# The feed-forward tail of a hybrid trunk block: eleven pairs of hidden tiles in chunks of 2, 3, 3 and 3, one plain pair, and operand blocks loaded by ScalarE

## The reference, cut to what matters

```python
h = _modulated_norm(x, norm_ffn_g[l], shift2, scale2)
hid = _causal_dwconv(h @ w_up[l], ffn_conv_w[l], ffn_conv_b[l])   # 1024 -> 6144, conv(3)
act, val = jnp.split(hid, 2, axis=-1)
x = x + gate2[:, None, :] * ((jax.nn.gelu(act) * val) @ w_down[l])   # 3072 -> 1024
return _rmsnorm(x, norm_final_g)
```

## Time and profile before

| | before |
|---|---|
| median of 3 runs | 1510.73 us |
| profiled execution | 1510.02 us |
| its span | 1508.3 us |
| PE busy | 1493.7 us (99%) |
| DVE busy | 1252.7 us (83%) |
| ACT busy | 819.4 us (54%) |
| POOL busy | 406.3 us (27%) |
| HBM read, written | 167.95 MB, 61.87 MB |
| clock granted to PE | 0.999 of full speed |

### The profile page before, as it was taken

One profiled execution on the slowest core, in us unless ns is written; L12 is line 12 of the kernel. 1 busy time (PEld: TensorE's weight loads), 2 busy tenths in 40 slices (PEclk: granted clock), 3 DMA queues, 4 the chain that ended last, 5 costly groups with the idle time before them and its releaser, 6 DMA issues.

```text
span 1508.3 us, 19815 instructions
## 1 busy us (share of the span) xinstructions
PE 1493.7 (99%) x6794; PEld 1233.5 (82%) x6794; DVE 1252.7 (83%) x1584; ACT 819.4 (54%) x1237; POOL 406.3 (27%) x313
## 2 busy tenths in 40 slices
PE   7999999999999999999999999999999999999998
PEld 5888888888888888888888878888888888888887
DVE  7987888777777786799869999999999987777776
ACT  5368888634454363423436555555555553444447
POOL 0033434522213223000101133333333331333325
PEclk9999999999999999999999999999999999999999
DMA  9432133373543364572520244444444436777722
GB/s 369 180 111 60 57 91 96 126 266 109 163 140 121 109 216 147 190 233 80 175 70 29 66 164 157 156 157 152 150 153 153 154 112 233 252 251 251 251 67 113
DMA packets 212227, 231.12 MB, mean 153 GB/s; under 512 B 9920, under 2 KB 164896, under 8 KB 211360
## 3 DMA queue, kind: packets, MB, share of 16 engines
...
HBM read 167.95 MB, written 61.87 MB: 152 GB/s over the span
## 4 chain that ended last, share of the span: by engine, by line
PE 94%; DVE 4%; ACT 1%; issue 0%; DMA 0%; DVEq 0%; ACTq 0%
PE ps L907 75%; PE ps L987 6%; PE ps L1008 2%; PE ps L1300 1%; PE ps L1146 1%; PE ps L1281 1%; PE ps L1058 1%; PE ps L1203 1%; PE ps L1104 1%; DVE wop L1984 1%; DVE hq L2644 1%; DVE hidw L2701 1%; DVE n L2636 0%; PE ps L1093 0%; PE ps L1330 0%; PE ps L808 0%
## 5 line engine op out<-in xcount | busy, mean ns | idle before, releaser
L1376 ACT ACTIVATE wop<-raw 128x512 fp32r<-128x512 f32 (+1 forms) x541 | 307.1, 571 | 345.1 <-PE ps L907 231.4
L1984 DVE TENSOR_TENSOR wop<-raw,wop 128x512 fp32r<-128x512 f32 (+1 forms) x541 | 377.6, 702 | 103.1 <-ACT wop L1376 101.5
L733 POOL TENSOR_TENSOR raw<-raw,raw 128x512 f32<-128x512 f32 (+1 forms) x69 | 100.0, 1450 | 858.2 <-DVE wop L1984 394.8
L907 PE MATMUL ps<-hq,wop 128*128 128x512 f32 x888 | 213.7, 390 | 0.2 <-DVE hq L2644 0.2
L907 PEld LDWEIGHTS ps<-hq,wop 128*128 128x128 f32 x888 | 166.4, 188 | 36.2 <-DVE hq L2644 1.0
L907 PE MATMUL ps<-yq,wop 128*128 128x512 f32 x792 | 191.3, 390 | 0.0
L907 PE MATMUL ps<-dq,wop 128*128 128x512 f32 x840 | 190.6, 389 | 0.0
L907 PEld LDWEIGHTS ps<-dq,wop 128*128 128x128 f32 x840 | 157.7, 188 | 32.7
L907 PEld LDWEIGHTS ps<-yq,wop 128*128 128x128 f32 x792 | 148.0, 188 | 30.7
L1998 DVE TENSOR_TENSOR ps<-ps,snap_p 128x512 f32<-128x512 f32 x136 | 94.6, 695 | 44.5 <-PE ps L907 43.9
L1391 ACT ACTIVATE snap_p<-ps 128x512 f32<-128x512 f32 x136 | 81.2, 597 | 82.7 <-PE ps L907 82.7
...
## 6 DMA issues: line engine op xcount, KB each, us to landing
dq<-hid_keep SPq DMA_DIRECT2D x35, 1024.0 KB, 7.0
...
raw<-in_w_down SPq DMA_DIRECT2D x80, 128.0 KB, 2.3
...
quarter_ring<-in_w_ada SPq DMA_DIRECT2D x64, 128.0 KB, 2.2
```

The costliest lines, as they stand in the source:

```text
L733: nc.gpsimd.tensor_tensor(s1, a21, a22, ALU.add).then_inc(s_made, 1)
L907: done = nc.tensor.matmul(bank, left[:, w, lk, :], right[:, x, rk, :], start=(first and w == 0 and x == 0), stop=(last and w == 1), skip_g ...
L1376: nc.scalar.activation(wop[n % 4][:, 0, 0:depth[n], :], raw[slot][:, 0:depth[n], :], ACT.Copy).then_inc(f_hi, 1)
L1984: V.tensor_tensor(wop[n % 4][:, 1, 0:kd, :], raw[slot_of[n][0]][:, 0:kd, :], wop[n % 4][:, 0, 0:kd, :].bitcast(F32), ALU.subtract).then_in ...
```

## The change

`NP`, the number of pairs that go through the seven-product scheme, goes from 10 to 11. M0 is gone. D has four chunks of 2, 3, 3 and 3 pairs and so 16 units: D0 to D3 with depth 2, D4 to D15 with depth 3 (9 matmuls a product). Tiles 20 and 21 are written to `hid_keep` as the eleventh pair. The tail of tile 23 (four conv taps, gelu, gate product, high and low part), which ran during M0, runs in D0, D1 and D2.

The buffers are seven `dq_first` of 1 MB for the first chunk and nine `dq` of 1.5 MB for the others. The loads of blocks are issued by ACT, between its own instructions, and no longer by SP. For chunks 2 and 3, two blocks are issued in the third unit of the chunk before and the other five in its fourth unit, each as soon as a product of that unit has released a buffer.

```diff
-        DK = 2
-        D_SIZE = 2 * DK * HALF * 4
-        D_AT = [("MY", 0), ("MY", 1), ("MH", 1), ("MH", 2), ("MH", 3), ("MY", 4), ("MY", 5),
-                ("MH", 4), ("MH", 5), ("MY", 2), ("MY", 3), ("MY", 6), ("MY", 7), ("MH", 6)]
-        D_FREED = (1, 1, 2, 3, 3, 4, 4, 5, 5, 6, 6, 7, 7)
-        dq = [place(f"dq{i}", [2, DK, HALF], F32, r, o * D_SIZE) for i, (r, o) in enumerate(D_AT)]
+        DK = 3
+        D_FIRST_AT, D_FIRST_FREED = (0, 8, 32, 40, 16, 24, 48), (1, 1, 4, 4, 6, 6, 7)
+        D_AT = [("MH", 8), ("MH", 20), ("MH", 32), ("MH", 44), ("MY", 0), ("MY", 36), ("MY", 12), ("MY", 24), ("MY", 48)]
+        D_FREED_U, D_FREED_D = (3, 3, 5, 7), (2, 4, 5, 6, 7)
+        dq_first = [place(f"dq_first{i}", [2, DK - 1, HALF], F32, "MY", o * KB) for i, o in enumerate(D_FIRST_AT)]
+        dq = [place(f"dq{i}", [2, DK, HALF], F32, r, o * KB) for i, (r, o) in enumerate(D_AT)]
+
+        def dq_of(c, i):
+            return dq[(7 * (c - 1) + i) % len(dq)] if c else dq_first[i]
...
-        NP = FT // 2 - 2
-        CHUNKS = [(c, c + DK) for c in range(0, NP, DK)]
-        SEQ += [("M", 0)] + [("D", (KT // 2) * c + i) for c in range(len(CHUNKS)) for i in range(KT // 2)] + [("L", 0)]
+        NP = FT // 2 - 1
+        CHUNKS = [(max(c, 0), c + DK) for c in range(NP % DK - DK, NP, DK)]
+        SEQ += [("D", (KT // 2) * c + i) for c in range(len(CHUNKS)) for i in range(KT // 2)] + [("L", 0)]
...
@@ SP @@
-                if (kind, u) == ("U", FT - 1):
-                    block_back(0, 0)
-                weights(pos, 2, 3)
-                if (kind, u) == ("U", FT - 1):
-                    block_back(0, 1)
-                    block_back(0, 2)
-                weights(pos, 3, 4)
+                if (kind, u) == ("D", 0):
+                    part_to_dram(NP - 1, "t4")
+                weights(pos, 2, 4)
+                if (kind, u) == ("D", 0):
+                    part_to_dram(NP - 1, "b22")
...
-                if (kind, u) == ("U", FT - 1):
-                    for i in range(3, 7):
-                        block_back(0, i)
-                if kind == "D" and u // 4 < len(CHUNKS) - 1:
-                    for i in range(2 * (u % 4), min(2 * (u % 4) + 2, 7)):
-                        block_back(u // 4 + 1, i)
...
@@ ACT @@
+            def block_back(c, i):
+                n = 7 * (c - 1) + i
+                k0, k1 = CHUNKS[c]
+                if c == 0:
+                    act.wait_ge(*used_at[first_op["U", FT - 1] + D_FIRST_FREED[i] - 1])
+                elif n < len(D_FREED_U):
+                    act.wait_ge(*used_at[first_op["U", FT - 1] + D_FREED_U[n] - 1])
+                    if n == len(D_FREED_U) - 1:
+                        act.wait_ge(part_lo, 7 * NP)
+                        act.wait_ge(part_out[1], 16 * PER_PAIR[1] * NP)
+                elif n < len(dq):
+                    act.wait_ge(*used_at[first_op["D", KT // 2 - 1] + D_FREED_D[n - len(D_FREED_U)] - 1])
+                else:
+                    c_before, i_before = divmod(n - len(dq), 7)
+                    act.wait_ge(*used_at[first_op["D", KT // 2 * (c_before + 2) - 1] + i_before])
+                if i == 0:
+                    for kind in range(3):
+                        act.wait_ge(part_out[kind], 16 * PER_PAIR[kind] * k1)
+                nc.scalar.dma_start(dq_of(c, i)[:, :, 0:k1 - k0, :], hid_keep[:, i, :, k0:k1, :]).then_inc(block_landed[i], 16)
+
+            def blocks_back(kind, u, w):
+
+                if (kind, u) == ("U", FT - 1):
+                    for i in range(7):
+                        if D_FIRST_FREED[i] == w:
+                            block_back(0, i)
+                if (kind, u, w) == ("D", 0, 0):
+                    block_back(0, D_FIRST_FREED.index(7))
+                if kind != "D" or u // (KT // 2) + 1 == len(CHUNKS):
+                    return
+                c, step = u // (KT // 2) + 1, u % (KT // 2)
+                ahead = 4 if c == 1 else 2
+                freed = D_FREED_D if c == 1 else range(1, 6)
+                if step in (1, 2) and w in (1, 4) and ahead - 4 + 2 * (step - 1) >= 0:
+                    block_back(c, ahead - 4 + 2 * (step - 1) + w // 4)
+                if step == 3:
+                    for i in range(ahead, 7):
+                        if freed[i - ahead] == w:
+                            block_back(c, i)
...
-                if kind == "M":
-                    tap(FT - 1, 1, pos - 1)
-                    gelu(FT - 1)
-                    hi(n0 + 3)
-                    hid_high(FT - 1)
...
+                    if (kind, u, w) == ("D", 0, 0):
+                        tap(FT - 1, 1, pos - 1)
                     if n0 + w + 3 < n_ops:
                         hi(n0 + w + 3)
+                    blocks_back(kind, u, w)
+                    if (kind, u, w) == ("D", 0, 6):
+                        gelu(FT - 1)
+                    if (kind, u, w) == ("D", 1, 6):
+                        hid_high(FT - 1)
...
@@ DVE @@
+                    if (kind, u) == ("D", 0) and w < 4:
+                        conv_tap(FT - 1, w // 2, w % 2 + 1, pos - 1)
+                    if (kind, u, w) == ("D", 1, 3):
+                        gate_mul(FT - 1)
+                    if (kind, u, w) == ("D", 2, 3):
+                        hid_low(FT - 1)
```

More of the change, by code:

```diff
@@ L337, in plain @@
         def plain(item):
-            return item[0] in "BML" or item in (("G", 0), ("O", 3)) or item[0] == "U" and item[1] < PLAIN
+            return item[0] in "BL" or item in (("G", 0), ("O", 3)) or item[0] == "U" and item[1] < PLAIN
         def row_of(t):
@@ L760, in _ @@
             for pos in range(NF + PLAIN, len(SEQ) - 1):
-                if SEQ[pos][0] != "M":
-                    weight_sums(SEQ[pos], (0,) if SEQ[pos] == ("U", PLAIN) else (0, 1))
+                weight_sums(SEQ[pos], (0,) if SEQ[pos] == ("U", PLAIN) else (0, 1))
             for i in range(NE - 1):
@@ L928, in unit @@
                 resident = YA_BLOCKS if item[0] == "A" else UP_BLOCKS if item[0] == "U" else NORM_BLOCKS
-                b11_, t1_, t2_, b22_, t3_, b21_, t4_ = resident if chunk is None else (dq[(7 * chunk + i) % len(dq)][:, :, :, :].bitcast(F32R) for i in range(7))
+                b11_, t1_, t2_, b22_, t3_, b21_, t4_ = resident if chunk is None else (dq_of(chunk, i)[:, :, :, :].bitcast(F32R) for i in range(7))
                 def t_ready(i):
@@ L1265, in _ @@
             quarter = [LB[0][:, 0, :], LB[0][:, 1, :], LB[1][:, 0, :], LB[1][:, 1, :]]
-            def middle_down(m, pos):
-                n0 = first_op["M", 0]
-                bank = BANKS[pos % 2][m % 2]
-                if m < 2:
-                    set_free(pos, m)
-                else:
-                    pe.wait_ge(down_used, m - 1)
-                for kk in range(2):
-                    n = n0 + 2 * (m // 4) + kk
-                    ready(n)
-                    pe.wait_ge(hid_lo, kk + 1)
-                    x_of = hid[hid_slot(2 * NP + kk)]
-                    for h in range(2):
-                        for w, x in PRODUCTS:
-                            done = nc.tensor.matmul(bank[:, h, :], wop[n % 4][:, w, m % 4, :], x_of[:, x, H[h]],
-                                                    start=(kk == 0 and w == 0 and x == 0), stop=(kk == 1 and w == 1))
-                done.then_inc(tile_done, 1)
             def last_down(i):
@@ L1306, in _ @@
                 kind, u = SEQ[pos]
-                if kind == "M":
-                    for m in range(KT):
-                        middle_down(m, pos)
-                elif kind == "D":
+                if kind == "D":
                     unit(pos, chunk=u // (KT // 2))
@@ L1863, in _ @@
                 j = u // 2 - 1
-                if kind == "M":
-                    tap(FT - 1, 1, pos - 1)
-                    gelu(FT - 1)
-                    hi(n0 + 3)
-                    hid_high(FT - 1)
-                    for n in range(n0 + 4, n0 + 7):
-                        hi(n)
-                    continue
                 for w in range(7):
```

62 lines of the change are left out of this document (13 added, 49 removed).

## The result

The changed kernel takes 1530.97 us (median of 4 runs, 1528.86 to 1533.07), beside 1510.52 for the kernel before in the same comparison: a ratio of 1.0132, 95% interval 1.0119 to 1.0144. It is slower by 20.5 us. The forecast was slower by 5, with a range that ended at 1520. The profiled execution took 1529.9 us, 19.9 above that of before (1510.02).

The account below looks back on a forecast made before the run. PE, busy 99%, bounds the kernel, so only fewer matmuls or new PE idle time count: 1510.02 - 2.72 + 2.5 (D0) + 2 x 2.5 (D8, D12) = 1514.8 us profiled, 1515.5 as median. Range 1509 to 1520.

Parts of the forecast that it names:

- The steady D stage: At D8 and again D12, block 6 lands after product 6 wants it: stall 1.2 to 3.9 us, taken as 2.5 each.
- T: Zero point of the forecast's times: start of D8 in the steady stage, start of D0's product in D0.
- in time: Before D4 only three blocks load in the last unit, landing 10.9 us after its start: no stall.
- Worse: Rival: blocks collide with SP's weight loads, a weight lands late; 1.5 us more per turn, D0 at upper end; 1521 us, chance 0.10.
- D0: Product 6 waits for DVE's second join (1.5 us) or block 6 (0.2 to 4.8 us); stall taken as 2.5 us.
- They catch up: nothing: D1 and D2 add 1.2 us to 6.6 of DVE work in a 9.52 us unit, costing nothing.
- the 12 matmuls: M0's pair costs 84 matmuls in the seven-product scheme instead of 96; PE saves 2.72 us.
- DVE's floor in D0: DVE's taps and low parts delay its second join, which product 6 needs: a stall of 1.5 us from DVE alone.
- ACT's issues: 28 block issues of 0.47, 13 us on ACT, cost PE nothing while ACT's high parts run three products ahead.
- the second queue gives no rate: ACT's and SP's DMAs share the same 16 engines; if ACT's queue added rate, D8's and D12's stalls would go.

Follow-up runs that it names:

- p_short_weights: The changed kernel with each D-stage weight load cut to one pair's weights (64 KB), blocks whole and issued by ACT; 1519.83 us, ratio 1.0058.
- g_wide_rows: The changed kernel with each D-stage weight load reading the same bytes from one contiguous stretch, in longer pieces; 1528.45 us, ratio 1.0124.
- b_sp_issues: The changed kernel with SP instead of ACT issuing the block loads, in one queue with the weight loads; 1520.09 us, ratio 1.0060.
- a_act_issues: The kernel before, with M0 and 14 buffers kept, but ACT instead of SP issuing the block loads; 1512.86 us, ratio 1.0017.
- c_short_blocks: The changed kernel with every block load, still issued by ACT, moving one pair only (512 KB); 1509.62 us, ratio 0.9993.

## Why the prediction was wrong

**The step that failed** is the fourth, "The steady D stage". It followed the blocks alone: "Block 6 lands at [...] T + 13.5 to 16.2 [...] The stall is 1.2 to 3.9 us", twice, and of D4 "in time". The weight loads beside the blocks were in the sum only as bytes that delay blocks, 0.47 to 0.9 us each, and never as something that PE waits for. They took up to 14.7 us. Each feeds a chain POOL, ACT, DVE, PE. The stall came at D4 (9.1 us with its slow clock) and was smaller at D8 and D12 (3.0 together, forecast 5.0). D4 was called safe by the same omission: at its turn only three blocks load, but two of them were issued at about the same time as the weights of its product 1. p_short_weights shows it for D4: with thin weights and whole blocks 10.6 of the 12.1 us are gone.

The blocks themselves behaved about as computed. At D8, block 6 was issued at 1372.3 and landed 14.7 later, at 1387.0, some 12.3 after D8's start; a late weight had by then delayed the unit's product 2 by 0.46, and PE did not wait for the block. At D12 it landed 14.2 after the unit's start (forecast 13.5 to 16.2), and product 6 came 1.4 us late by it (forecast 1.2 to 3.9). So the mechanism of the fourth step is real, at one of the two turns and at its low end, and g_wide_rows shows it at both; it is 1.4 of the 12.1 us, and what the step left out is most of the rest.

**The rival that had the mechanism** was "Worse": a weight lands late and POOL's sums follow late. Its price, 1.5 us in each turn, was worked out from nothing that a full queue had shown, and with a chance of 0.10 and an end at 1521 it was both too cheap and too unlikely. The 2.3 us median of the earlier trace rows was of loads that shared one queue with the blocks, at most two blocks at a time; b_sp_issues and a_act_issues put the price of the second queue at 10.9 and 2.4 us. The Trainium skill, "DMA: Bandwidth & Descriptors", has both rules that were needed. I cited the one, that issuing engines are not separate DMA queues in rate; the traces agree: two queues moved 423 GB/s from 1379.4 to 1382.4, and SP's queue alone 423 in b_sp_issues from 1360 to 1366. The other, in its section "Queues, rings and completion order", is that a DMA engine takes turns between the queue rows that have work. I did not draw its consequence: an issue on a second queue is not behind the weight loads but beside them. The price of 2.0 us plus bytes over 436 GB/s, which the prediction takes from the same page of the Trainium skill, is given there for DMAs that GpSimd issues; the block loads here are SP's and ACT's, and the sum did not use it.

**D0** was mis-sized, not misjudged. The second join ended 9.5 us after T, forecast 9.65, and block 6 landed at T + 11.4, inside 8.4 to 13.0. PE started product 6 at T + 11.45 instead of T + 8.16, 3.3 us, forecast 2.5 (the profile puts that row's gap down to issue, but it starts 0.1 us after block 6 has landed). I stopped there. D0 to D3 lost 8.6: the weights of D0 to D2 had been caught in the same crowd (9.03, 6.11, 5.00 us), and the clock was at its lower level after the gap. "They catch up: nothing" held for DVE alone; c_short_blocks lost 2.3 us over the four units, of which the gap is 1.27 and the rest is not explained.

**U23** was not in the sum at all, and lost 1.8 us. The forecast had SP's writes of the eleventh pair as traffic that delays block 6, but not as a thing that ACT waits for before it can reuse the part buffer.

**The clock** was not in the sum: about 1.4 us after D4's gap, and of that order after D0's.

**What was right**: the 12 matmuls (6794 to 6782 in the page's first part; with their 2.72 us the ledger closes to 0.1 us); DVE's floor in D0; that ACT's issues, 0.37 to 0.50 us each, cost PE nothing that c_short_blocks could show; that the second queue gives no rate.

**What stays open**: how an engine divides its turns between the two queues (tripling the pieces of one side changed its longest wait only from 12.3 to 9.7 us); how the 3.0 us at D8 and D12 would split if only the weights, and not the blocks, came sooner; and how much of the 7.8 us that D0 to D3 lose with SP as issuer is D0's crowd and how much the order of SP's list. A kernel that spreads U23's writes and the first chunk's loads over more units was not tried.
